# A three-block network on one core: attention rows by pairs of heads with the mask added in the maximum, and recurrence cells split into a front and a back

## The reference

```
# block 1, for each chunk, per head, in both directions (state C, n, m)
s = einsum('bhtd,bhsd->bhts', qb, kb) * w_intra
num = einsum('bhts,bhsv->bhtv', s, vb) + w_inter[..., None] * einsum('bhtd,bhdv->bhtv', qb, C)
den = s.sum(-1) + w_inter * einsum('bhtd,bhd->bht', qb, n)
h = num / maximum(abs(den), exp(-m_t))[..., None]
C_new = decay[..., None, None] * C + einsum('bhs,bhsd,bhsv->bhdv', wk, kb, vb)

# block 2: q and k of a head have 128 plain columns and 64 rotary ones; k's rotary part is shared by all heads
q_pe = apply_rope(q_pe, cos, sin)
s = einsum('bqhd,bkhd->bhqk', qi, kf) * scale
s = where(kpos <= qpos, s, -inf)
p = softmax(s)
o = einsum('bhqk,bkhd->bqhd', p, v)
```

## Time and profile before

| what | value |
|---|---|
| time, median of 3 runs | 4738.52 us (4734.31 to 4741.97) |
| time of the profiled execution | 4737.19 us |
| its span in the profile | 4735.4 us |
| TensorE busy | 4526.5 us, 96% |
| VectorE, ScalarE, GpSimd busy | 1678.8, 908.1, 687.9 us |
| cells of the recurrence, in the span | 357.4 to 509.5 us |
| heads of the attention, in the span | 1722.4 to 2164.6 us |

### The profile page before, as it was taken

How to read it: one execution, slowest core, us unless ns; L and a number is a source line. 1 busy time by engine, 2 the same in 40 slices (tenths; PEclk the granted TensorE clock), 3 DMA queues, 4 the chain that set the end, 5 groups by cost and what they waited for, 6 DMA issues and landing times.

```text
span 4735.4 us, 38254 instructions
## 1 busy us (share of the span) xinstructions
PE 4526.5 (96%) x15556; PEld 2437.0 (51%) x15556; DVE 1678.8 (35%) x2628; ACT 908.1 (19%) x1635; POOL 687.9 (15%) x581
## 2 busy tenths in 40 slices
PE   6998899999999999999999999899999999999999
PEld 3457444444444455555444444754599744444444
DVE  4233363333325113232698422534433332222100
ACT  2113230000002112221232211433244310000000
POOL 3002006333200000000263100000121003112000
PEclk8999899999999999999999999999999999999999
DMA  4410001111110100000100111001000121111101
GB/s 173 160 44 1 18 18 45 45 45 45 45 36 33 36 31 12 12 18 20 43 36 36 45 71 38 22 30 40 22 1 1 54 89 45 45 45 42 75 37 60
DMA packets 50490, 202.37 MB, mean 43 GB/s; under 512 B 5632, under 2 KB 7168, under 8 KB 49168
## 3 DMA queue, kind: packets, MB, share of 16 engines
q1 hardware_dynamic: 46656, 168.58, 9.9%
q0 software_dynamic: 3664, 31.41, 1.7%
HBM read 185.29 MB, written 14.68 MB: 42 GB/s over the span
## 4 chain that ended last, share of the span: by engine, by line
PE 90%; DVE 5%; ACT 2%; issue 1%; DMA 1%; POOL 1%; SPq 0%; DVEq 0%; ACTq 0%; POOLq 0%; PEldq 0%
PE bank L183 34%; PE bank L463 24%; PE bank L2139 6%; PE bank L2337 6%; PE bank L1412 2%; PE bank L1439 1%; PE bank L1443 1%; PE bank L1461 1%; PE bank L2086 1%; PE bank L2067 1%; PE bank L2166 1%; PE bank L1418 1%; PE bank L297 1%; PE bank L2315 1%; DVE ABC L2561 1%
## 5 line engine op out<-in xcount | busy, mean ns | idle before, releaser
L183 PE MATMUL bank<-H,ring 128*128 128x512 f32 x2624 | 1141.9, 597 | 32.4 <-DMA ring<-in_proj 20.6
L183 PEld LDWEIGHTS bank<-H,ring 128*128 128x128 f32 x2624 | 500.7, 191 | 663.0 <-issue 624.5
L183 PE MATMUL bank<-ABC,ring 128*128 128x512 f32 x1264 | 550.2, 596 | 4.9 <-POOL ABC L1372 2.6
L183 PEld LDWEIGHTS bank<-ABC,ring 128*128 128x128 f32 x1264 | 239.8, 191 | 304.5 <-issue 297.4
L2337 PE MATMUL bank<-ABC,ring 128*128 128x512 f32 x704 | 303.9, 595 | 2.6 <-PEq L2325 2.6
L463 PE MATMUL bank<-H,ring 128*128 128x512 f32 x576 | 253.1, 592 | 0.0
L1727 DVE SCALAR_TENSOR_TENSOR bank<-ABC,params,bank 128x1024 f32<-128x1024 f32 x184 | 237.3, 1290 | 8.0
L2337 PEld LDWEIGHTS bank<-ABC,ring 128*128 128x128 f32 x704 | 134.3, 191 | 172.2 <-issue 168.8
L463 PEld LDWEIGHTS bank<-H,ring 128*128 128x128 f32 x576 | 109.4, 190 | 137.8 <-issue 137.8
L1357 POOL TENSOR_TENSOR ABC<-ABC 128x1024 f32<-128x1024 f32 x48 | 113.4, 2363 | 220.3 <-ACT ABC L1570 214.6
L463 PE MATMUL bank<-H,X 128*128 128x512 f32 x304 | 136.8, 592 | 0.7 <-POOL H L762 0.7
(11 more groups left out here) (483 smaller groups left out, 6103.6 us busy)
## 6 DMA issues: line engine op xcount, KB each, us to landing
ABC<-in_ada SPq DMA_DIRECT2D x48, 512.0 KB, 6.3
ring<-in_gu SPq DMA_DIRECT2D x44, 512.0 KB, 4.1
ring<-in_up SPq DMA_DIRECT2D x32, 512.0 KB, 4.3
ring<-in_down SPq DMA_DIRECT2D x32, 512.0 KB, 4.3
ring<-in_conv_in SPq DMA_DIRECT2D x24, 512.0 KB, 4.3
ring<-in_ffn SPq DMA_DIRECT2D x16, 704.0 KB, 4.8
ring<-in_proj SPq DMA_DIRECT2D x16, 512.0 KB, 6.6
ring<-in_mix SPq DMA_DIRECT2D x16, 512.0 KB, 4.5
```

Source lines behind the costliest of these rows:

```text
L183: mm = nc.tensor.matmul(bank[:, 2 * (m % 2) + h, :], ring[:, s % RING, k * P:(k + 1) * P], rhs(k)[:, h * HALF:(h + 1) * HALF], start=(k == ...
```

## The change

**Recurrence.** A cell has a front (mask, weights, `bcast`, values, scores, keys) and a back (`out`, `state`). TensorE, ScalarE and VectorE do the front of the next cell before the back of this one. `values`, `queries`, `keys_tok` and `probs_t` exist twice (`probs_t` lies in `norm_room`). The values are turned straight from A, without GpSimd's copy. The keys are turned by 2 transposes from A in place of 4 products of 64 columns from the block-diagonal tile. GpSimd copies a cell's keys once `scores` of the cell two before is done. GpSimd's sum of the third pair of chunks (6 and 1) now stands behind the whole loop and waits for the last cell's output.

**Attention.** The rotary rows of two heads (64 each) are made by one set of products, turned once, and kept for both. The second head reads them with `k_pes[1]`, a copy of the shared rotary keys whose first 64 rows are zero; in `k_pes[0]` the last 64 are zero. GpSimd makes both. The rotary rows come first and the rotation before `k` and `v`. The mask is no longer a product: `tensor_tensor_reduce` on VectorE adds a mask row of up to 1024 columns to the scores, writes the sum to SBUF and gives the maximum; a `tensor_scalar` on 1 column negates it. The exponential works in SBUF in place. The blocks run in the lengths 8, 1, 7, 2, 6, 3, 5, 4, with the scores two blocks ahead; long ones use banks 0, 1 (scores) and 4, 5 (transposes), short ones banks 2 and 3. The mask table `mla_const` grows from 2 to 9 blocks of 128 columns.

```diff
+            for n in range(CELLS):
+                i, d, c, now = cell_of(n)
+                if n >= 2:
+                    pool.wait_ge(*cell_pe.after(0, f"scores{n - 2}"))
+                for e, name in enumerate(("low", "high")):
+                    rows = slice(64 * e, 64 * e + 64)
+                    nc.gpsimd.tensor_copy(keys_bd[rows, d, e::2, :], A[rows, 2:4, now]).then_inc(*cell_pool.did(f"{name}{n}"))
...
+                if n in (13, 15):
+                    head_sums_of(n // 2 - 1)
+            head_sums_of(7)
...
+            def cell_front(n):
+                i, d, c, now = cell_of(n)
+                if n:
+                    pe.wait_ge(*cell_act.after(0, f"weights{n - 1}"))
+                nc.tensor.matmul(bank[:, 0, :], ident[:, :], causal[:, d:d + 1, :].broadcast_to([P, 4, P]),
...
+                for h in range(4):
+                    mm = nc.tensor.transpose(bank[:, 2, h * P:(h + 1) * P], A[:, 4 + h, now], ident[:, :])
+                mm.then_inc(*cell_pe.did(f"values{n}"))
+                pe.wait_ge(*cell_pool.after(0, f"high{n}"))
+                if n:
+                    pe.wait_ge(*cell_dve.after(0, f"probs{n - 1}"))
...
+                pe.wait_ge(*cell_dve.after(0, f"queries{n}"))
+                for q in range(2):
+                    mm = nc.tensor.transpose(bank[:, 1, 256 + q * P:256 + (q + 1) * P], A[:, 2 + q, now], ident[:, :])
+                mm.then_inc(*cell_pe.did(f"keys{n}"))
+
+            def cell_back(n):
+                i, d, c, now = cell_of(n)
+                pe.wait_ge(*cell_dve.after(0, f"probs{n}"))
+                if n:
+                    pe.wait_ge(*cell_act.after(0, f"out{n - 1}"))
+                if n >= 2:
+                    pe.wait_ge(*cell_dve.after(0, f"state{n - 2}"))
...
+            for n in range(-1, CELLS):
+                if n + 1 < CELLS:
+                    cell_front(n + 1)
+                if n >= 0:
+                    cell_back(n)
...
+            LENGTHS = [7, 0, 6, 1, 5, 2, 4, 3]
...
+            p_exp = lambda g: p_small[:, g // 2 % 2, :] if g % 2 else Hf[:, (1 + g // 2 % 2) * SEQ:(2 + g // 2 % 2) * SEQ]
+            k_pes = [k_pe, Hf[:, 6 * SEQ:7 * SEQ]]
+            score_bank = lambda g: bank[:, 2, :] if g % 2 else two_banks(0)
+            turn_bank2 = lambda g: bank[:, 3, :] if g % 2 else two_banks(4)
...
+                if e == 0:
+                    rows("pe", 4, 7, 3, 0)
+                rows("q", 0, 0, 3, 0)
+                if e == 0:
+                    pe.wait_ge(*now(mla_act, "pe"))
+                    for h in range(2):
+                        mm = nc.tensor.matmul(bank[:, 4 + h, :], rot, q_raw[:, h * HALF:(h + 1) * HALF], start=True, stop=True)
+                    mm.then_inc(*mla_pe.did("rot_0"))
+                rows("k", 2, 3, 2, 3)
...
+                        if n >= 2:
+                            pe.wait_ge(*now(mla_dve, f"max{n - 2}"))
...
+                        v.wait_ge(*now(mla_pe, f"s{n}"))
+                        nc.vector.tensor_tensor_reduce(p_exp(n)[:, 0:(b + 1) * P], score_bank(n)[:, 0:(b + 1) * P],
+                                                       causal_row[:, (NT - 1 - b) * P:], 1.0, -3e38, ALU.add, ALU.max,
+                                                       one(row_max)).then_inc(*mla_dve.did(f"max{n}_{e}"))
+                        v.wait_ge(*now(mla_dve, f"max{n}"))
+                        nc.vector.tensor_scalar(one(neg_max), one(row_max), -1.0, None, ALU.mult).then_inc(*mla_dve.did(f"neg{n}_{e}"))
```

More of the change, by code:

```diff
@@ L539, in build, with in_turn @@
             cell_zero = steps("cell_zero", "zeroed")
[L540 to L544, removed]
+            CELLS = 2 * NT
+            def in_turn(first, second):
+                return " ".join(" ".join([f"{what}{n + 1}" for what in first if n + 1 < CELLS] + [f"{what}{n}" for what in second if n >= 0])
+                                for n in range(-1, CELLS))
+            cell_pool = steps("cell_gpsimd", " ".join(f"low{n} high{n}" for n in range(CELLS)))
+            cell_pe = steps("cell_tensor", in_turn(("bcast", "values", "scores", "keys"), ("out", "state")))
+            cell_act = steps("cell_scalar", in_turn(("weights", "keys"), ("out",)))
+            cell_dve = steps("cell_vector", in_turn(("queries", "values", "probs"), ("neg", "guard", "den", "recip", "state")))
             ripe = [4, 3, 5, 2, 6, 1, 0, 7]
@@ L1197, in b1_vector @@
-                for c in ripe[2 * (i - 5):2 * (i - 5) + 2] if i >= 5 else []:
-                    v.wait_ge(*head_pool.after(0, f"sum{c}"))
-                    head_stat(c)
+                    last.then_inc(*cell_dve.did(f"state{n}"))
+                    for ready in {12: ripe[0:2], 14: ripe[2:4], 15: ripe[4:6]}.get(n, ()):
+                        v.wait_ge(*head_pool.after(0, f"sum{ready}"))
+                        head_stat(ready)
             head_recip("early", 0, 6, "std_early")
-            v.wait_ge(*cell_act.all(lead=1))
+            v.wait_ge(*cell_act.all())
@@ L1471, in b2_tensor @@
             pe.sem_inc(*mla_pe.lead())
-            for i in range(8):
-                head(t0 + i, i, t0 + i)
+            for pair in range(4):
+                for e in range(2):
+                    head(pair, e)
             pe.wait_ge(*mla_dve.all(lead=1))
```

462 lines of the change are left out of this document (222 added, 240 removed).

## The result

The changed kernel takes **4657.02 us** (median of 4 runs, 4652.55 to 4657.38) where the one before takes 4737.83 (4 runs beside it): a ratio of 0.9827, interval 0.9816 to 0.9838. The forecast was 4661.

A forecast was written before the change was run, and what follows sets the result against it. TensorE was taken to bound the kernel, gaining only from less work or shorter waits. 4737.2 - 30.9 (cells) - 46.7 (attention) = 4659.6, plus 1.3 to the runs' median, stated as 4661 us; 8-in-10 range 4647 to 4681.

The forecast's parts named there:

- The cells, forecast -30.9: Recurrence stage: cells of 6.83 us where 8.69 stood, with start and tail costs, net 30.9 us less.
- The first stretch at half clock: Start of the cells: TensorE runs at 1.2 GHz as before the change, costing 6.4 us.
- the 1.0 of the memsets: Ahead of the first cell: TensorE waits for two more GpSimd memsets of 0.5 us each, 1.0 us.
- The late sum on GpSimd: End of the cells: sums of chunks 6 and 1 wait for the last output, adding 1.3 us to the path.
- The attention, work removed: Attention on TensorE: rotary rows 20.6, rotations 6.9 and mask records 13.8 go, together 41.3 us.
- The attention, waits: Attention on TensorE: old waits of 41 us give way to 4.9 per head, 39 in all: 2 us less.
- the 0.4 at the seven-block product: Attention, each head: the seven-block product with the values waits for its copy, mostly covered, 0.4 us.
- The clock, forecast one stretch left in the attention: Attention: of three half-clock stretches of 1.7 us each, one stays, so 3.4 us less.
- The unknown price: VectorE's reduction with PSUM source, SBUF mask and SBUF output: taken as 1290 ns for 1024 columns.
- the first rival: Attention: the reduction streams at half rate, 2.36 us for 1024 columns, 26 us in all, total 4687 us; chance 0.07.
- rival 2: Cells: a late semaphore keeps a wait of 1.0 us per cell, 16 in all, total 4677 us; chance 0.09.
- rival 3: Attention: two close waits above 1 us send TensorE to 1.2 GHz in most heads, 12 us more, 4673; chance 0.09.

The follow-up runs named there:

- the sequential run: Changed kernel with each cell's front directly ahead of its own back on all three engines; 4665.3 us, ratio 0.9843.
- e1_attention_only: Kernel before with the attention part of the change alone, cells as before; 4686.4 us, ratio 0.9888.
- e5_rotary_twice: Changed kernel whose second heads again make the rotary rows and rotation, results unused; 4683.3 us, ratio 0.9880.
- e9_reduction_twice: Changed kernel with a plain maximum over the same scores, result unused, ahead of every VectorE reduction; 4698.6 us, ratio 0.9913.
- e6_rotation_late: Changed kernel with the rotation moved behind the values, as before, in the four first heads; 4671.6 us, ratio 0.9855.
- e2_cells_only: Kernel before with the recurrence part of the change alone, attention as before; 4703.8 us, ratio 0.9922.

## Why the prediction was right

**The cells, forecast -30.9, measured -33.1 for the start of `mix`.** The working of a cell held: 6.83 forecast, 6.77 measured, with no new wait in the common cell. What was removed was named rightly, and the sequential run shows that the crossing gives 0.7 to 0.8 of the 1.9 us, less than the 1.0 and 0.15 that the working put down to the waits, since the keys alone in their new place already cover part. The first stretch at half clock was kept at 6.4 us and cost about 4.5 by the distances of the masks: it ended 9.3 us behind the first mask, not 14.9. That is luck and no work of the change, since with the cells of before it ended after 8.6 in `e1_attention_only`. Against that run's cells the stage is 31.6 us shorter, where the forecast, without the 1.0 of the memsets ahead of the first mask, says 31.9. The second half-clock stretch lies behind the cells and took back some: it was 13.7 us long before, and now TensorE ran at 1.2 GHz in the 24 us up to the start of `mix` and just past it,

```profile
477.00:501.00 24.00, 9.80 (x24) 5.82 (x25) 10.53 (x51) 13.03 (x34) 0.45 (x1) 0.50 0.00 0
```

and from `mix` to the attention 1.3 us more were spent. The late sum on GpSimd was forecast at 1.3; its own piece is 1.27, and what the wait for the last output costs in the tail is 1.6.

**The attention, work removed, forecast 41.3.** The rotary part is shown (27.4 for 27.5 forecast, `e5_rotary_twice`). The mask's 13.8 is right as work (12.9 of busy time) and not as gain: 8.9, as its products filled waits.

**The attention, waits, forecast 2 us less.** This term was mis-sized. With 41.3 of work and 3 x 1.7 = 5.1 of clock taken off, 6.1 of the 52.5 us are left for waits, so a head waits some 4.4 us and not 4.9. The listed rows give 24.2/8 = 3.0 of it (the five above and two single ones), 0.15 behind each modelled end 0.8 more, and the last 0.6 would be waits too short to be listed; that is argued, not shown. Of the forecast places all but one were found: the 0.4 at the seven-block product is in no listed row. Counted from the last issue, as the forecast counts, the sizes were 1.05 for 1.2, 0.82 for 1.1, and 1.9 for 2.2 at the end. The heads took 52.15 and 45.29 us, for 52.7 and 45.8.

**The clock, forecast one stretch left in the attention.** None was left: 1.7 us more gained. Outside of the two stages the forecast had no term, and 5.3 us more were spent there in the profiles. These errors of opposite sign (2.2 + 5.8 against 5.3) let the total come out 2.8 us from the forecast span, nearer than its parts. Part of it goes together: the stretches at 1.2 GHz add up to 144 and 140 us over the two spans, so what the clock gave in the two stages it took back in the others. That the parts came out so near each other is luck.

**The unknown price.** The reduction from PSUM with an SBUF mask takes 1226 ns for 1024 columns, the lower bound of the earlier trace rows, and 84 ns more to read the accumulator, 1.31 us together, near the 1290 that I took. Half rate, the first rival, is excluded for this mix of places. `e9_reduction_twice` bears on what it would have cost: it adds 1.23 us per 1024 columns where the rival had 1.07, and the listed waits grew by 26 us, with 8.5 from the clock on top; the rival's 26 had no clock in it, and the expectation of that run, 37, was for waits alone. By the Trainium skill, "Vector Engine (DVE) Microarchitecture Reference", section "Points that are easy to get wrong", the halving is stated for `S2S2D2_STT` with two sources in SBUF that are not bf16. The prediction set this rule against its own step, but there one source lies in PSUM, so the 1226 ns don't test it. The 1284 ns of the earlier trace rows have both sources in SBUF and show no halving; the trace lists both reductions as CUSTOM_DVE_ANT_0, and whether the rule is meant for them no run here shows.

**The other rivals.** The cells don't keep a wait (rival 2): in one of them the keys wait 0.23 us for `queries`, and that cell is 0.45 longer than the others, where the forecast had 0.6 for the statistics; the last back waits 1.19 us for VectorE's L1215, where it had 1.3. The waits of 0.88 and 0.66 never brought the half clock (rival 3), while in `e9_reduction_twice` waits of 2.0 and 1.7 close together did so in five of eight heads, and in `e6_rotation_late` waits of 2.78 in four of four. Rival 3 did not come about, but longer waits at the same places show its mechanism.

## What to carry to other kernels

Work removed from the engine that sets the end is worth its full time only where nothing is waited for just behind it; measure it by putting it back, as the mask gave 8.9 of 13.8 us and the rotary rows 27.4 of 27.5. When blocks of unequal length share an engine, look at the first two as well as the last: the third block's scores need the first one's reduction over, so another order, with a middle-sized block first, gave 12.9 us in one line. Price a wait of some 2 to 3 us on TensorE by what follows it too, and judge small edits by their own stage, since the rest of a long kernel can move by 5 us with the clock. Before a loss in an untouched stage is put down to a change, compare it with the spread of one kernel's executions, here up to 12 us, and the clock over the whole span.

## What the runs showed of the hardware

- A wait of TensorE of 2.7 to 2.8 us was followed by 3.4 us at 1.2 GHz in 3 of 8 heads before, 2 of 8 in `e2_cells_only` and 4 of 4 (evenly spaced) in `e6_rotation_late`; two waits of 2.0 and 1.7 us close together in 5 of 8. Each time it cost 1.7 us. Waits of up to 0.88 us in the attention were followed by none.
- Stretches at 1.2 GHz change places between executions with the same work: the first one in the cells of before ended 14.9 us behind the first mask in one profile and 8.6 in another, and the 8952 records behind the attention took 2570.8 to 2579.5 us. That an edit in one stage causes such a loss in another is not shown.
- Engines far from full hold TensorE back by when they are late: VectorE at 42% of the attention in `e9_reduction_twice` cost 26 us of waits for 48 us of work.
